# A hybrid attention and expert block on one core: low parts of the output weights on VectorE alone, first linear-attention states and read-out inside the attention loop

## The chip, the cores and the metric

The kernel runs on one core of a Trainium2 chip. The metric is the device time in microseconds of one execution. PE is TensorE, ACT is ScalarE, DVE is VectorE, POOL is GpSimd and SP is SyncE, whose queue issues most of the loads.

## What is computed

One layer of a residual block over 1024 tokens of width 1024, all in 32-bit floats:

```python
u = rms_norm(h, g1);  proj = u @ w_in          # split into sq sk sv | gq gk gv gr glr
sb = stick_breaking_attention(norm(sq), norm(sk), sv)     # 8 heads x 64, causal, blocks of 128 queries
sb = rms_norm(sb, sb_out_norm_g)
# gated linear attention, 4 heads, key 64, value 128, chunks of 64 tokens:
S = exp(total) * S + k_dec.T @ v ;  o = q @ S              # S is carried from chunk to chunk
go = rms_norm(o, gla_out_norm_g) * silu(gr)
h = h + concat(sb, go) @ w_out
h = h + hierarchical_moe(rms_norm(h, g2))                  # 32 experts, two for each token
```

## The kernel before, in words

Each engine has a program of its own, written in order by hand; only semaphores tie them together. A large product is made from high and low parts, so that one product is three matmuls: for each weight W, `W_h = round(W)` is made by ScalarE and `W_l = W - W_h` by VectorE or GpSimd.

**Stages.** (1) Norm and transposes of x, then the projection in 40 units. (2) The attention loop: 48 steps (`steps_z`, NZ = 48), n = 0 to 47. Query tile i has 4 pairs of heads, and one (i < 4) or two steps a pair; tile 7 has steps 40 to 47, each 512 keys wide. Software pipelining runs the engines some steps apart: in iteration n TensorE does `scores(n)`, `turn_a(n-2)` and `values(n-3)`; ScalarE two sigmoids of step n and the copy of the probabilities of step n-2; VectorE two scans and one product of step n. In the gaps `fill` makes the query and gate columns (12 units, the last one in iteration 39). (3) The output projection, 8 tiles of 128 tokens: each with 8 steps k of 6 matmuls (`three` for two halves). Between the steps stand small works: the state of the linear attention (`keys_values(t, c)` on TensorE, `next_state(n)` on VectorE, n = 2t + c), its read-out (`read_state`), the transposes of its output (`turn_gla`) and of the attention output (`turn_sb`), and of the tile before `turn_h`, `route` and `rank_tile`. (4) The experts, 32 or more blocks: six pieces of 1 MiB of weights each, split into high and low parts by ScalarE (`high`, line 1419) and VectorE (`low_piece`, line 1527), then 96 matmuls.

**Output weights.** SyncE loads w_out in four parts into raw slots 1, 2, 3 and again 1 (`load_wo`, line 421), once the fill is done. ScalarE makes wo_h in iterations 41, 42, 43 and 45 (`WO_SPLIT`). GpSimd makes wo_l of parts 0 and 1 (line 582: multiply two rows by a gain; line 584: one subtraction of 128 x 2048), VectorE that of parts 2 and 3 (`wo_low`, line 1611: two fused instructions of 128 x 1024).

**End of the loop.** Bank 6 collects the attention output of every tile; `values` of a new tile waits until ScalarE's `evict_o` has emptied it. After the loop TensorE runs: keys_values(0, 0), keys_values(0, 1), both read_state(0, c), turn_sb(0), keys_values(1, 0), turn_gla(0), keys_values(1, 1), and then the projection of tile 0. VectorE answers with next_state(0), next_state(1), go_mean(0), and so on. GpSimd waits for the last scores, clears the three states, then loads gv_in 0 and 1 and gate_in and scales all eight rows of the attention output (`norm_sb`, line 602).

**Weight pieces.** There are six raw slots and two extra, and six split slots. SyncE issues pieces 0 to 5 behind the stores of tiles 0 to 5 (waits `v_ready`), then waits for all scatters of rows by expert (`own_scattered`, line 469), then issues piece 6 and so on, each when the piece that held its slot has been split (`ew_l_ready`). Pieces 12 and 13 lie where the rows of the last tiles lay. After tile 7 the engines build block 0 from rows in memory and rows still at hand (`first_rows`, `add_rows`) and run gate_up(0).

**In tile 7 of the projection** (w = 7 on VectorE and ScalarE) stand the routing of tile 6 (`take_logits`, `choose`, `rank_tile(6)` behind k = 6, `place_tile(6)`). ScalarE makes the high parts of pieces 0 and 1 after it, VectorE the low part of piece 0 between place_tile(6) and `add_h(7)` (line 1698).

## Time and profile before

| | |
|---|---|
| three runs, median (lowest to highest) | 1273.97 us (1273.42 to 1276.81) |
| the profiled execution | 1275.61 us |
| its span, first to last instruction | 1273.8 us |
| mean granted TensorE clock | 0.971 of full |
| busy: PE, DVE, ACT, POOL | 1192.8, 871.7, 734.2, 297.8 us |
| chain that ended last: PE, DMA, DVE, ACT, issue | 68%, 17%, 6%, 5%, 3% |

The rows below come from that one execution. A timeline line gives start and duration in microseconds, engine, line of the kernel, operation, out<-in, shapes and count; what stands in brackets is the idle time of the engine before it and what ended that. A granted clock of 1.00 is 2.4 GHz, 0.50 is 1.2 GHz. Where two instructions of an engine overlap in a group, the group's time is the stretch they cover.

### The profile page before, as it was taken

To read this page: it belongs to the slowest core of one execution; us is meant where nothing else is said; L and a number is where in the kernel's file an instruction comes from. 1 tells how busy PE (TensorE), PEld (TensorE's weight loads), DVE (VectorE), ACT (ScalarE), POOL (GpSimd) and SP (SyncE) were. 2 spreads that over 40 slices of the span, in tenths; PEclk is the share of its full clock that TensorE was granted. 3 is DMA by queue.
4 is the path that set the end of the run, shared out by engine and by line. 5 is a ranking of instruction groups with operands and counts; after the bars stand their busy time and mean duration, and the time that the engine had idled before them with its cause. 6 is when DMAs were issued, how large, how long until landed. Compare 5 with 4: busy or idle time off the path is not lost.

```text
span 1273.8 us, 17673 instructions
## 1 busy us (share of the span) xinstructions
PE 1192.8 (94%) x6172; PEld 976.1 (77%) x6172; DVE 871.7 (68%) x987; ACT 734.2 (58%) x894; POOL 297.8 (23%) x256
## 2 busy tenths in 40 slices
PE   4999999999999968999978999999999999999993
PEld 3897777877767746777866888888788888888883
DVE  5721212267556696577668999888888888888880
ACT  4532222266455583223245887887778777878870
POOL 3400000010000074033232333334344222232210
PEclk9999999999999987999988999999999999999997
DMA  7145432020000122356639999999999999999961
GB/s 255 43 162 219 151 139 108 1 67 17 18 12 23 57 93 88 111 209 231 254 135 385 371 378 383 377 372 372 368 374 378 370 379 374 372 379 390 379 241 15
DMA packets 67828, 288.12 MB, mean 226 GB/s; under 512 B 13008, under 2 KB 20193, under 8 KB 43202
## 3 DMA queue, kind: packets, MB, share of 16 engines
q1 hardware_dynamic: 51538, 238.30, 49.1%
q0 software_dynamic: 10864, 30.29, 8.6%
q10 hardware_dynamic: 5376, 18.88, 3.8%
q8 instruction: 30, 0.49, 0.2%
q14 instruction: 20, 0.16, 0.0%
HBM read 242.79 MB, written 48.25 MB: 228 GB/s over the span
## 4 chain that ended last, share of the span: by engine, by line
PE 68%; DMA 17%; DVE 6%; ACT 5%; issue 3%; SPq 0%; ACTq 0%; POOL 0%; POOLq 0%; DVEq 0%
PE banks L746 17%; DMA raw<-in_expert_w_up 16%; PE banks L747 16%; PE banks L748 16%; PE banks L886 4%; DVE ew_l L1527 3%; PE banks L853 3%; ACT ew_h L1419 2%; PE banks L870 2%; PE banks L974 1%; DVE tails L1630 1%; PE banks L1066 1%; PE banks L919 1%; PE banks L933 1%; DMA x_in<-in_x 1%
## 5 line engine op out<-in xcount | busy, mean ns | idle before, releaser
L1527 DVE TENSOR_TENSOR ew_l<-raw,ew_h 128x2048 fp32r<-128x2048 f32 x192 | 437.9, 2290 | 64.1 <-ACT ew_h L1419 62.9
L1419 ACT ACTIVATE ew_h<-raw 128x2048 fp32r<-128x2048 f32 x192 | 368.1, 1919 | 122.2 <-DMA raw<-in_expert_w_up 50.5
L746 PE MATMUL banks<-ew_h,xb_h 128*128 128x512 f32 x512 | 204.2, 399 | 12.2 <-issue 6.8
L748 PE MATMUL banks<-ew_h,xb_l 128*128 128x512 f32 x512 | 201.1, 393 | 0.0
L747 PE MATMUL banks<-ew_l,xb_h 128*128 128x512 f32 x512 | 201.0, 393 | 0.0
L1630 DVE TENSOR_TENSOR_SCAN tails<-tails 128x512 f32<-128x512 f32 (+3 forms) x96 | 103.2, 1117 | 63.8 <-ACT tails L1314 63.7
L746 PE MATMUL banks<-win_h,u_h 128*128 128x512 f32 (+1 forms) x320 | 123.7, 387 | 0.1
L746 PEld LDWEIGHTS banks<-ew_h,xb_h 128*128 128x128 f32 x512 | 97.3, 190 | 34.2 <-issue 14.5
L747 PE MATMUL banks<-win_l,u_h 128*128 128x512 f32 (+1 forms) x320 | 120.4, 376 | 0.0
L748 PE MATMUL banks<-win_h,u_l 128*128 128x512 f32 (+1 forms) x320 | 119.9, 375 | 0.0
L748 PEld LDWEIGHTS banks<-ew_h,xb_l 128*128 128x128 f32 x512 | 97.1, 190 | 20.9
L747 PEld LDWEIGHTS banks<-ew_l,xb_h 128*128 128x128 f32 x512 | 97.1, 190 | 19.3
L746 PE MATMUL banks<-ew_h,a_h 128*128 128x512 f32 x256 | 103.1, 403 | 2.2 <-DVE a_l L1527 2.2
L747 PE MATMUL banks<-ew_l,a_h 128*128 128x512 f32 x256 | 100.6, 393 | 0.0
L748 PE MATMUL banks<-ew_h,a_l 128*128 128x512 f32 x256 | 100.6, 393 | 0.0
L695 POOL DMA_INDIRECT out_dram<-y_row,scatter_row x32 | 46.6, 1457 | 175.6 <-issue 175.6
L574 POOL TENSOR_TENSOR z_l<-z_raw,z_h 128x1024 fp32r<-128x1024 f32 x6 | 14.6, 2440 | 306.1 <-ACT z_h L1250 306.1
L1314 ACT ACTIVATE tails<-banks 128x1024 f32<-128x1024 f32 (+3 forms) x48 | 39.3, 818 | 74.7 <-PE banks L857 59.4
L685 POOL DMA_INDIRECT xb<-rows_dram,gather_idx x30 | 65.7, 2189 | 52.3 <-issue 50.4
L886 PEld LDWEIGHTS banks<-v_s,prob 128*128 128x128 f32 x576 | 73.5, 199 | 5.1 <-issue 2.2
L886 PE MATMUL banks<-v_s,prob 128*128 128x64 f32 x576 | 72.2, 277 | 2.0 <-ACT o_sb L1302 2.0
L746 PEld LDWEIGHTS banks<-win_h,u_h 128*128 128x128 f32 x320 | 61.3, 192 | 12.8 <-issue 2.9
(242 smaller groups left out, 2023.7 us busy)
## 6 DMA issues: line engine op xcount, KB each, us to landing
raw<-in_expert_w_gate SPq DMA_DIRECT2D x64, 1024.0 KB, 12.0
raw<-in_expert_w_up SPq DMA_DIRECT2D x64, 1024.0 KB, 8.4
raw<-in_expert_w_down SPq DMA_DIRECT2D x64, 1024.0 KB, 12.7
rows_dram<-zero_rows ACTq DMA_DIRECT2D x8, 2048.0 KB, 7.6
win_raw<-in_w_in SPq DMA_DIRECT2D x16, 512.0 KB, 5.3
x_in<-in_x SPq DMA_DIRECT2D x8, 512.0 KB, 9.9
raw<-in_w_out SPq DMA_DIRECT2D x4, 1024.0 KB, 5.9
h_row<-in_x SPq DMA_DIRECT2D x8, 512.0 KB, 6.3
```

The lines of the kernel that those rows point to most:

```text
L685: pool.indirect_dma_start(out=xb[0:n, :], out_offset=None, in_=rows_dram, in_offset=bass.IndirectOffsetOnAxis(ap=gather_idx[0:n, :], axis= ...
L695: pool.indirect_dma_start(out=out_rows, out_offset=bass.IndirectOffsetOnAxis(ap=scatter_row[0:n, 0:1], axis=0), in_=y_row[0:n, :], in_offs ...
L746: mm(ps, lh, rh, start=start, stop=False)
L747: mm(ps, lh, rl, start=False, stop=False)
L748: return mm(ps, ll, rh, start=False, stop=stop)
L853: last = mm(z[h], q_t[row, u["i"], u["pair"], :], k_t[row, u["pair"], u["lo"]:u["lo"] + u["w"]], start=True, stop=True)
L870: last = nc.tensor.transpose(bank[4 + h][:, P * j:P * j + P], beta[n % 3][:, h, P * j:P * j + P], ident[:, :])
L886: last = mm(bank[6][:, SB_DIM * hd:SB_DIM * (hd + 1)], prob[n % 2][:, h, P * j:P * j + P], v_s[:, u["lo"] // P + j, SB_DIM * hd:SB_DIM * ( ...
L1314: A(tails[u["row"] % 2][:, :, u["col"]:u["col"] + u["w"]], z, ACT.Sigmoid, scale=-1.0).then_inc(c_done, 1)
L1419: A(ew_h[slot % SPLIT][:, :], raw[raw_slot][:, :], ACT.Copy).then_inc(ew_h_ready, 1)
L1527: return V.tensor_tensor(dst, src, high.bitcast(fp32), SUB)
L1630: last = V.tensor_tensor_scan(out=part, data0=part, data1=part, initial=1.0 if u["top"] else row[:, h, c1:c1 + 1], op0=MUL, op1=ALU.min)
```

## The change

1. **wo_l on VectorE alone.** The GpSimd loop is gone; VectorE makes all four parts. The parts are in raw slots 1, 2, 1, 2; ScalarE and VectorE split them in iterations 41, 42, 44 and 45. SyncE loads two parts at once and the others when VectorE is done with the slot. Raw slot 3's memory is thus free and takes the three states and gv_in 0.
2. **Linear attention in the loop.** keys_values(0, 0) goes behind iteration 44 of TensorE, keys_values(0, 1) behind 45 (it waits for next_state(0)), both read_state(0, c) behind 47. next_state(0) and next_state(1) stand at the ends of iterations 45 and 46 on VectorE. These use bank 6; the attention output of the last tile is collected in bank 7. ScalarE does go_square(0) and go_rstd(0) in iterations 48 and 49 and evict_o(7) after sb_high(0).
3. **Start of the projection.** Before tile 0 stand only turn_sb(0), turn_gla(0) and keys_values(1, 0); keys_values(1, 1) goes behind k = 1, read_states(1) behind k = 2, keys_values(2, 0) behind k = 3.
4. **GpSimd** clears the states and loads gv_in 0 when the fill is done; norm_sb(t + 1) is done in turn t of its loop, after load_gate(t), instead of all at once.
5. **First pieces.** The high and the low part of piece 0 are made in turn w = 7, the low part ahead of take_logits(6). SyncE's wait for the scatters moves from before piece 6 to before piece 12; piece 5 waits for the last read-out (g_o), as its slot holds the states.

```diff
-        WO_SPLIT = {FILL_LAST + d: n for n, d in enumerate((2, 3, 4, 6))}
+        WO_SPLIT = {FILL_LAST + d: n for n, d in enumerate((2, 3, 5, 6))}
+        WO_SLOT = (1, 2, 1, 2)
...
@@ SyncE
-            for n in range(3):
+            for n in range(2):
                 load_wo(n)
             store_gate(2 * GLA_HEADS - 1)
-            sp_e.wait_ge(wo_l_ready, 1)
-            load_wo(3)
+            for n in range(2, 4):
+                sp_e.wait_ge(wo_l_ready, n - 1)
+                load_wo(n)
...
+                if t == 5:
+                    sp_e.wait_ge(g_o, 2 * TILES)
                 if t < 6:
                     load_piece(raw_slot(t), gate_up(t // 4, t % 4))
...
-            for k in range(2):
-                sp_e.wait_ge(own_scattered[k], 32 * TILES // 2)
             for j in range(2, 6):
                 sp_e.wait_ge(ew_l_ready, j - 1)
...
                 if m == 12:
                     sp_e.wait_ge(x_turned, 1)
                     for k in range(2):
+                        sp_e.wait_ge(own_scattered[k], 32 * TILES // 2)
                         sp_e.wait_ge(v_stored[k], 16 * TILES // 2)
@@ GpSimd
-            for n in range(2):
-                pool.wait_ge(wo_h_ready, n + 1)
...
-                nc.gpsimd.tensor_tensor(wo_l[:, 2 * n:2 * n + 2, :], src[:, :, :], wo_h[:, 2 * n:2 * n + 2, :].bitcast(fp32),
-                                        SUB).then_inc(wo_l_ready, 1)
...
-            pool.wait_ge(qk_done, NZ)
-            for i in range(3):
+            pool.wait_ge(fill_done, FILL_UNITS)
+            nc.gpsimd.memset(state[2][:, :, :], 0.0)
+            for i in range(2):
                 last = nc.gpsimd.memset(state[i][:, :, :], 0.0)
             last.then_inc(prepared, 1)
             for i in range(2):
                 pool.wait_ge(gv_stored[i], 16 * TILES // 2)
+            load_gv(0)
+            pool.wait_ge(qk_done, NZ)
+            load_gv(1)
             pool.wait_ge(gate_stored, 16 * 2 * GLA_HEADS)
-            load_gv(0)
-            load_gv(1)
             load_gate(0)
-            for t in range(TILES):
-                norm_sb(t)
+            norm_sb(0)
+            norm_sb(1)
...
                 load_gate(t)
+                if t + 1 < TILES:
+                    norm_sb(t + 1)
@@ TensorE
+            GLA_EARLY = {NZ - 4: lambda: keys_values(0, 0), NZ - 3: lambda: keys_values(0, 1), NZ - 1: lambda: read_states(0)}
...
                 if n >= 3:
                     values(n - 3)
+                if n in GLA_EARLY:
+                    GLA_EARLY[n]()
...
-            keys_values(0, 0)
-            keys_values(0, 1)
-            for c in range(2):
-                read_state(0, c)
             turn_sb(0)
+            turn_gla(0)
             keys_values(1, 0)
-            turn_gla(0)
-            keys_values(1, 1)
...
+                    if t == 0 and k == 1:
+                        keys_values(1, 1)
+                    if k == (0 if t else 2) and t + 1 < TILES:
+                        read_states(t + 1)
...
-                    if k == 2 and t + 2 < TILES:
+                    if k == (2 if t else 3) and t + 2 < TILES:
                         keys_values(t + 2, 0)
@@ ScalarE
+                    go_square(0)
+                if n == NZ + 1:
+                    go_rstd(0)
...
-            go_square(0)
-            go_rstd(0)
             sb_high(0)
+            evict_o(TILES - 1, NZ - 1)
+            go_high(0)
...
+                if w == TILES - 1:
+                    act.wait_ge(g_mixed, TILES)
+                    high(0, 0, raw_slot(0), raw_count(0), guard=False)
@@ VectorE
-                if WO_SPLIT.get(n, 0) >= 2:
+                if n in WO_SPLIT:
                     wo_low(WO_SPLIT[n])
+                if NZ - 3 <= n < NZ - 1:
+                    next_state(n - (NZ - 3))
...
                 if r >= 0:
                     norm_h(r)
+                if w == TILES - 1:
+                    low_piece(0, 0, raw_slot(0))
+                if r >= 0:
                     take_logits(r)
...
             place_tile(TILES - 2)
-            low_piece(0, 0, raw_slot(0))
             add_h(TILES - 1)
```

## Rows read from the trace of the kernel before

**Rows 1.** Timeline, VectorE in the last attention steps: start us, us, what.
```profile
450.57 1.23 DVE L1635 TENSOR_TENSOR beta<-beta,tails 128x1024 f32<-128x1024 f32 x1
...
456.89 0.67 DVE L1623 TENSOR_REDUCE o_ms<-o_sq 128x8 f32<-128x512 f32 x1
...
458.19 7.12 DVE L1630 TENSOR_TENSOR_SCAN tails<-tails 128x512 f32<-128x512 f32 x2 [0.63 <-ACT tails L1314]
...
469.74 6.64 DVE L1630 TENSOR_TENSOR_SCAN tails<-tails 128x512 f32<-128x512 f32 x2
...
481.19 2.47 DVE L1611 SCALAR_TENSOR_TENSOR wo_l<-raw,mix_gain,wo_h 128x1024 fp32r<-128x1024 f32 x2
...
487.09 2.45 DVE L1630 TENSOR_TENSOR_SCAN tails<-tails 128x512 f32<-128x512 f32 x2
...
489.58 1.23 DVE L1635 TENSOR_TENSOR beta<-beta,tails 128x1024 f32<-128x1024 f32 x1
...
496.11 1.43 DVE L1659 SCALAR_TENSOR_TENSOR state<-state,gstat,banks 64x128 f32<-64x128 f32 x4 [5.30 <-PE banks L919]
```

**Rows 2.** The same timeline, GpSimd.
```profile
457.70 4.53 POOL L584 TENSOR_TENSOR wo_l<-raw,wo_h 128x2048 fp32r<-128x2048 f32 x1
...
492.24 7.03 POOL L602 TENSOR_TENSOR o_sb<-o_sb,o_rs 128x512 f32<-128x512 f32 x7 [3.85 <-ACT o_rs L1338]
```

**Rows 3.** The same timeline, TensorE and one ScalarE eviction.
```profile
477.70 1.97 PE L870 MATMUL banks<-ident,beta 128*128 128x128 f32 x8 [6.97 <-DVE beta L1635]
...
482.90 2.08 PE L853 MATMUL banks<-k_t,q_t 64*128 64x512 f32 x4
...
485.03 1.03 ACT L1314 ACTIVATE tails<-banks 128x1024 f32<-128x1024 f32 x1 [4.30 <-PE banks L853]
...
486.39 1.90 PE L886 MATMUL banks<-v_s,prob 128*128 128x64 f32 x16
...
495.40 0.65 PE L919 MATMUL banks<-gv_in,k_dec 64*64 64x128 f32 x8
...
507.35 0.79 PE L746 MATMUL banks<-wo_h,mix_h 128*128 128x512 f32 x1
```

**Rows 4.** Busy time and granted clock: us, PE, PEld, DVE, ACT, POOL, PEclk, DMA share, GB/s.
```profile
477.00:486.00 9.00, 8.30 (x33) 6.68 (x34) 8.93 (x9) 2.00 (x3) 0.95 (x3) 0.50 0.00 0
```

**Rows 5.** Timeline, a read-out inside tile 0 of the output projection.
```profile
510.12 1.09 PE L933 MATMUL banks<-state,gq_t 128*64 128x256 f32 x8
```

**Rows 6.** Timeline of the last tiles before the experts, 628 to 668 us.
```profile
635.65 0.22 DVE L1715 SCALAR_TENSOR_TENSOR grp_logits<-banks,stat,router_bias 128x4 f32<-128x4 f32 x1 [2.49 <-PE banks L974]
...
641.68 2.33 DVE L1527 TENSOR_TENSOR ew_l<-raw,ew_h 128x2048 fp32r<-128x2048 f32 x1
...
643.93 1.27 DVE L1698 TENSOR_TENSOR h_row<-h_row,banks 128x512 f32<-128x512 f32 x2
```

**Rows 7.** Waits of the DMA queue of SyncE, 640 to 720 us: total, times, longest.
```profile
SPq L469 <- DMA rows_dram<-v_row,dest: 19.4, 1, 19.4
```

**Rows 8.** Stretches of 4 us: length, granted clock, DMA share, GB/s.
```profile
658.00:662.00 4.00, 1.00 0.00 0
...
670.00:674.00 4.00, 0.95 0.94 359
```

**Rows 9.** Raw weight loads issued from 462 to 463 us: issue to landing.
```profile
DMA to landing us min/median/max: 4.7/4.7/4.7
```

**Rows 10.** Raw weight loads issued from 712 to 718 us: issue to landing.
```profile
DMA to landing us min/median/max: 7.3/7.3/7.3
```

**Rows 11.** Raw weight loads issued from 856 to 874 us: issue to landing.
```profile
DMA to landing us min/median/max: 12.4/12.9/13.4
```

**Rows 12.** The chain that ended last, whole span: start us, us, what.
```profile
699.42 0.88 PE banks L1066 x8
...
823.69 0.88 PE banks L1066 x8
...
1133.89 0.88 PE banks L1066 x8
```

More of the change, by code:

```diff
@@ L1607, in wo_low @@
                 dve.wait_ge(wo_h_ready, n + 1)
-                src = raw[(1, 2, 3, 1)[n]][:, :].rearrange("p (k n) -> p k n", n=D)
+                src = raw[WO_SLOT[n]][:, :].rearrange("p (k n) -> p k n", n=D)
                 for kk in range(2):
@@ L1612, in wo_low, with next_state @@
                                                   in1=wo_h[:, k, :].bitcast(fp32), op0=MUL, op1=SUB)
-                last.then_inc(wo_l2_ready, 1)
+                last.then_inc(wo_l_ready, 1)
+            def next_state(n):
+                t, c = divmod(n, 2)
+                kv_bank = bank[7 if t else 6]
+                dve.wait_ge(g_kv, n + 1)
+                if n == 0:
+                    dve.wait_ge(prepared, STATES)
+                else:
+                    dve.wait_ge(g_state, n)
+                if n >= 3:
+                    dve.wait_ge(g_o, n - 2)
+                for p in range(2):
+                    for h in range(2):
+                        r, col = slice(64 * h, 64 * h + 64), slice(GLA_V * h, GLA_V * (h + 1))
+                        last = V.scalar_tensor_tensor(out=state[n % 3][r, p, col], in0=state[(n - 1) % 3][r, p, col],
+                                                      scalar=gstat[r, t, 2 * p + c:2 * p + c + 1],
+                                                      in1=kv_bank[r, GLA_V * p:GLA_V * (p + 1)], op0=MUL, op1=ADD)
+                last.then_inc(g_state, 1)
             dve.wait_ge(unit_done, UNITS)
@@ L1771, in place_tile, with low_piece @@
                 dve.wait_ge(dest_ready, 2 * (t + 1))
-            next_state(0)
-            next_state(1)
+            def low_piece(count, slot, raw_slot):
+                dve.wait_ge(ew_h_ready, count + 1)
+                low(ew_l[slot % SPLIT][:, :], raw[raw_slot][:, :], ew_h[slot % SPLIT][:, :]).then_inc(ew_l_ready, 1)
             go_mean(0)
+            go_norm(0)
+            sb_low(0)
+            go_gate(0)
+            go_low(0)
+            next_state(2)
             dve.wait_ge(o_squared, TILES)
             V.reduce_sum(o_ms[:, TILES - 1, :], heads(o_sq[:, :]), axis=AX.X).then_inc(o_mean, 1)
-            go_norm(0)
-            sb_low(0)
-            next_state(2)
-            go_gate(0)
-            go_low(0)
             next_state(3)
```

155 lines of the change are left out of this document (65 added, 90 removed).

## The prediction, made before the changed kernel was run

> **What bounds the kernel now.** I read the chain that ended last first, because it says which wait counts in which stage, then the timeline around the places that the diff touches, then the waits and landings of the loads. Three stages have three limits. In the last attention steps the chain runs over VectorE: a step costs it two scans and a product, 3.72 us from 487.09 to 490.81, yet two pairs of scans took 7.12 and 6.64 us where a free pair takes 2.45 [rows 1]. Each lies on a 4.5 us GpSimd subtraction for wo_l (one of two in [rows 2]). TensorE stands idle behind that for 6.97 us and then runs at half clock (0.50 from 477 to 486 us [rows 3, 4]). From the last values matmul, 495.4, to the first output-projection matmul, 507.35, is 11.9 us of short dependent work for one tile [rows 3]. The projection itself is bound by TensorE. The experts are bound by TensorE at first, 17.75 us a block from 699.42 to 823.69 (7 blocks), then by the weight loads, 18.25 us a block from 823.69 to 1133.89 (17 blocks), with the load as the link before the split [rows 12]. Ahead of the experts the DMA engines stand still (0.00 at 658 us [rows 8]) while SyncE waits 19.4 us for row scatters before it issues piece 6 [rows 7].
>
> **The change part by part.** All sums are against the profiled execution: span 1273.8, 1275.61 in all, which is 1.6 above the median 1273.97 of the three runs. I take the difference off the median.
>
> *VectorE in the loop.* I start at 451.80, the end of the product of step 41 [rows 1]. To the product of step 47, at 490.81, it took 39.0 us: six steps at 3.72 (22.3), two wo_low at 2.47 (4.9), one head sum 0.67, and 11.1 of hindrance, of which the two long scan pairs are 4.7 + 4.2. Without GpSimd's part the hindrance goes. The work becomes six steps 22.3, four wo_low 9.9, head sum 0.7, two state updates at 1.43 [rows 1] 2.9: 35.8 us. The raw reloads for wo_low 2 and 3 are hidden: they are issued at 454.3 and 460.5, land 4.7 later [rows 9] and are wanted by VectorE at 468.6 and 474.8; if they came 5 us late they would cost what remains, nothing.
>
> *The new wait.* After step 45 TensorE waits for next_state(0), which VectorE reaches only after scan, product and wo_low(3) of that step. Queued behind the wait is scores(46), and for that wait ScalarE's eviction and VectorE's scan of step 46. The ledger puts next_state(0) at 477.3 to 478.7. TensorE's last work before is values(42), ended about 467.5, so it idles 11 us, and I take the half clock that followed the 6.97 us idle. Then keys_values(0,1) 1.0 (a row of 0.65 at full clock [rows 3], 1.0 at half), scores 2.08 and its mask 0.3, eviction 1.03 [rows 3]: VectorE starts step 46 at 483.2, 4.5 us of bubble. Step 46 and next_state(1) end at 488.3. scores(47) waits on TensorE for turn_a(44) 1.97 and values(43), 3.3 at half clock (1.90 at full [rows 3]), so it starts at 487.4 and its eviction ends at 489.5: bubble 1.2. The product of step 47 ends at 493.2, 2.4 later than before, although 11.1 us of hindrance are gone. No row shows which clock TensorE has after 11 us idle: at full clock both bubbles shrink to 3.0 in all and the loop ends some 4 us earlier than put here, at half clock to its end it is rival 3; I go by the nearest row, 6.97 us idle and then half clock to about 486.
>
> *End of the loop.* Before, from scores(47) at 482.90 to 495.4 TensorE worked without a gap for 12.5 us, 1.6 of it excess of the half clock. Now 487.4 + 10.9 + 1.1 for read_states(0) (1.09 [rows 5]) = 499.4. ScalarE puts go_square(0) before the last copy of probabilities, 0.6, mostly under values(46). The loop ends 4.0 later.
>
> *Hand-over to the projection.* Gone from it are both keys_values of tile 0, both state updates, the read-out, square, mean and scale. Left, by the rows that exist: turn_sb(0) 0.5 to 0.6 (four transposes; eight took 1.97 at half clock), its copy 0.6 and evict_o(7) 1.1 (one and two evictions of 512 columns; 1024 took 1.03), keys_values(1,0) 0.65 [rows 3], and 0.15 of hand-overs: 3.1 us, so the first projection matmul comes at 502.5 instead of 507.35: **4.9 us**. GpSimd's three memsets, moved to the end of the fill, stand in free time. load_gv(0) is issued 40 us earlier; load_gate(0) and norm_sb(0) stand behind load_gv(1) as before. norm_sb(0) is ready at 497, turn_sb(0) wants it at 499.4.
>
> *Tile 0 of the projection.* keys_values(1,1) (0.65) moves in, read_states(1) goes behind k=2. The state of chunk 3 is ready when it is read, the one of chunk 4 about 0.3 late. Against that stands less half clock: the first six matmuls took to 510.12, 2.8 us, and cost 1.4 at full clock [rows 3, 5]. From +0.9 to -0.9; I take 0.
>
> *Tile 7.* high(0) and low(0) of the first expert go before take_logits(6), which started at 635.65; low takes 2.33 and ends at about 637.1, so the logits come 1.4 late, and rank_tile(6) holds TensorE's last six matmuls by 1.3. But add_h(7), which waited for that low piece from 641.68 to 643.93 [rows 6], starts at about 642.8: **1.1 us** won, between -1.3 and 2.3. SyncE's wait for g_o = 16 at t = 5 costs nothing: the last read-out lies in tile 6 before norm_h(5).
>
> *Piece loads.* SyncE no longer waits for the scatters. Pieces 6 and 7 go out at about 648 and 650 instead of 668.7, piece 8 at 664, piece 9 at 669 (its split has not moved). Three pieces of 1.05 MB at the 359 GB/s of 670 to 674 us [rows 8] are 8.8 us of DMA time taken out of the queue. That is not the gain: the ring of raw buffers allows no more issues ahead, and by 712 us a load lands 7.3 us after issue [rows 10] where one into idle engines took 4.7 [rows 9]. Only 2.6 us of backlog are there to remove; after that the engines go idle. Later the landing grows to 12.9 [rows 11] and the blocks stretch; 17 blocks lost 17 x (18.25 - 17.75) = 8.4 us [rows 12], and a backlog 2.6 smaller puts the onset off by as much. I take **2.4**, between 0 and 8.4.
>
> Sum: 4.9 + 0 + 1.1 + 2.4 = 8.4 us, 1273.97 - 8.4 = **1265.6**.
>
> **A rule on ports.** The long scans waited until GpSimd's subtraction had ended, and a GpSimd multiplication beside them did far less. The Trainium skill, "SBUF — State Buffer", section "Who interferes with whom", says why: a VectorE instruction with two SBUF inputs and a GpSimd one that reads SBUF exclude each other for a whole instruction. By that rule, the trace agrees on the scans. It also speaks against this change, which moves six norm_sb into the projection: rival 4.
>
> **The rivals.**
> 1. *The head start of the loads is lost* (0.20): transfers drain to the same backlog by the point where blocks stretch. For it: the DMA share is already 0.94 at 670 us [rows 8], so the megabytes behind meet a queue all the same. 1273.97 - 6.0 = 1268.0.
> 2. *The head start counts in full* (0.10), since bound by loads is bound by their first byte. Against it: the 7.3 us landing. 1273.97 - 6.0 - 8.4 = 1259.6.
> 3. *Slower: the half clock stays* (0.07). TensorE idles 11 us instead of 7 in the loop. If it does not return by 487, each microsecond at the lower level costs about half of one; the gain is gone when it lasts some 17 us longer, and lasting 27 longer, to tile 0, costs 13.5: 1279.1. Against it: after 6.97 us idle the half clock was over by 486.39, where 16 values matmuls took 1.90 again [rows 3].
> 4. *GpSimd blocks VectorE in the projection* (0.10). Before, all but the last norm_sb ran in one stretch at 492.24, 7.03 us for seven [rows 2]; now norm_sb 2 to 7 stand one to a tile, 1.0 each: up to 6 us, 1271.6, no measurable change. Against it: the state updates at 496.11 ran at full speed beside them [rows 1], and TensorE, not VectorE, is full in this stage. The skill's page named above would make it so for go_low and norm_h, which have two SBUF inputs.
> 5. *The loop does not give what it promises* (0.08): the wait for next_state(0) costs twice the 5.7 of bubble that I put, as the pipeline of three engines must fill again. 1265.6 + 5.7 = 1271.3.
>
> **How the numbers follow.** Forecast 0.45, with 1263 to 1268 as its own range (tile 0 by 0.9 either way, tile 7 by 1). About 0.3%, 3.8 us, is what a measurement can tell from no change: 1270.2 and 1277.8 are the marks. Faster: forecast, rivals 1 and 2, and 0.02 of 4 and 5, 0.77. Same: the rest of 4 and 5, 0.16. Slower: rival 3, 0.07. The range 1258.5 to 1271.5 takes in rivals 1, 2 and 5 and the full-clock case (some 1261.6), and leaves out rival 3, the upper end of 4, and what I have not seen, 0.2 in all.
>
> **What would show it.** Scan pairs in steps 42 to 47 all near 2.45 and no subtraction on GpSimd; TensorE idle about 11 us before keys_values(0,1); the first projection matmul near 502.5; add_h(7) without a low piece before it; DMA engines busy from 648 to 656 us; landings near 5 us at block 2, with blocks stretching some five later than now. The prediction is wrong if the loop ends after 503, if loads land in 7 us again at block 2, or if the tiles of the projection grow longer than before.

## The result, and the profile after

The changed kernel takes 1265.62 us, the median of 5 runs (1261.56 to 1266.81), against 1273.97 for the kernel before beside it, also 5 runs (1272.15 to 1276.81): a ratio of 0.993, 95% interval 0.9909 to 0.9951. The forecast was 1265.6. Its sum agrees with the result, but most of its terms do not. Two large ones were wrong in opposite directions, and a microsecond and a half came from a stage that nobody changed. One execution of experiment e9 below took 1974.52 us at a granted clock of 0.557 and is left out of its median and ratio.

The profiled execution took 1266.81 us, with a span of 1265.1 and a mean granted clock of 0.976 (before: 1275.61, 1273.8, 0.971). The rest of this document compares stages by the starts of the same instructions in both traces: first scores matmul of step 40, first matmul of the output projection, its last matmul of wo_h with mix_h (two more follow it, up to 0.9 us later, and then add_h of tile 7 can start), first matmul of `first_rows`, `turn_rows` of block 2, last matmul. What the stages sum to in the profiled execution, and what the prediction had for each:

| stage | before | after | difference | forecast |
|---|---|---|---|---|
| start to step 40 | 442.12 | 440.50 | -1.6 | 0 |
| step 40 to the first projection matmul | 65.23 | 56.78 | -8.45 | -4.9 |
| projection, tile 0 | 16.01 | 15.61 | -0.4 | 0 |
| projection, tiles 1 to 6 | 103.10 | 107.29 | +4.2 | 0 (rival 4: up to +6) |
| tile 7, and to `first_rows` | 25.04 | 23.42 | -1.6 | -1.1 |
| `first_rows` to block 2 | 47.76 | 48.73 | +1.0 | 0 |
| block 2 to the last matmul | 556.84 | 555.00 | -1.8 | -2.4 |

**The start.** The difference arises ahead of step 0 of the loop, where nothing is changed, and most of it in one place: TensorE ran at half clock from 209.6 to 213.0 us in the kernel before, and at full clock at the same work in the changed one. Windows as in [rows 4], kernel before, then changed:

```profile
209.00:213.00 4.00, 4.00 (x12) 3.11 (x11) 0.42 (x1) 0.31 (x2) 0.00 (x0) 0.57 0.38 127
```

```profile
208.00:212.00 4.00, 3.95 (x19) 3.38 (x20) 0.43 (x1) 0.47 (x3) 0.00 (x0) 1.00 0.69 196
```

**The end of the loop.** VectorE of the changed kernel, timeline (start, duration, what), to be read against [rows 1]:

```profile
458.98 2.45 DVE L1653 TENSOR_TENSOR_SCAN tails<-tails 128x512 f32<-128x512 f32 x2
...
474.53 1.42 DVE L1633 SCALAR_TENSOR_TENSOR state<-state,gstat,banks 64x128 f32<-64x128 f32 x4
480.56 2.34 DVE L1653 TENSOR_TENSOR_SCAN tails<-tails 128x512 f32<-128x512 f32 x2 [4.60 <-ACT tails L1329]
...
485.65 2.46 DVE L1653 TENSOR_TENSOR_SCAN tails<-tails 128x512 f32<-128x512 f32 x2
```

All pairs of scans take 2.33 to 2.46 us where two had taken 7.12 and 6.64, and GpSimd does no arithmetic until 491 us. The state update ends at 475.95, and the idle 4.60 ahead of the scans of step 46 is the bubble (forecast 4.5). The scans of step 47 follow on the second update without a hole; the forecast had 1.2 there. TensorE, against [rows 3]:

```profile
476.01 1.12 PE L904 MATMUL banks<-gv_in,k_dec 64*64 64x128 f32 x8 [10.30 <-DVE state L1633]
...
479.25 1.25 PE L865 MATMUL banks<-ident,beta 128*128 128x128 f32 x8
480.34 1.90 PE L884 MATMUL banks<-v_s,prob 128*128 128x64 f32 x16
...
494.38 0.61 PE L960 MATMUL banks<-ident,o_sb 128*128 128x128 f32 x4
...
497.28 0.50 PE L741 MATMUL banks<-wo_h,mix_h 128*128 128x512 f32 x1
```

TensorE idles 10.30 us for the state update (forecast 11), and keys_values(0, 1) behind it takes 1.12 instead of 0.65. From 479.25 on the groups are short again: 1.25 for a turn that takes 1.97 at half clock, then 1.90 for a `values` of 16. The granted clock by windows, in the columns of [rows 4]:

```profile
470.00:474.00 4.00, 0.00 (x0) 0.00 (x0) 3.97 (x4) 0.00 (x0) 0.00 (x0) 0.50 0.00 0
474.00:478.00 4.00, 1.99 (x10) 1.22 (x12) 1.91 (x5) 0.00 (x0) 0.00 (x0) 0.50 0.00 0
478.00:482.00 4.00, 4.00 (x30) 2.94 (x26) 1.44 (x2) 2.50 (x3) 0.00 (x0) 0.79 0.00 0
```

The clock is down for about 10 us, but TensorE works at it only from 476.0 to some 479.5. In the kernel before it worked 8.3 us at that level, 477.7 to 486, behind a hole of 6.97 us [rows 3, 4].

**The projection.** Waits of TensorE for other engines from tile 1 to the end of tile 6 (total, times, longest):

```profile
PE banks L989 <- DVE chosen_any L1749: 3.6, 4, 0.9
```

In the kernel before nothing was waited for in these tiles. L989 is `rank_tile`, which wants `chosen_any` (line 1749), the last result of `choose`. One such place on the timeline, VectorE:

```profile
547.48 1.56 DVE L1734 TENSOR_SCALAR r_small<-iota,r_small 128x4 f32<-128x4 f32 x1
...
550.91 0.18 DVE L1749 TENSOR_TENSOR chosen_any<-chosen 128x32 bf16<-128x32 bf16 x1
```

and GpSimd:

```profile
547.95 1.06 POOL L593 TENSOR_TENSOR o_sb<-o_sb,o_rs 128x512 f32<-128x512 f32 x1
```

A VectorE comparison of 4 elements a partition takes 1.56 us: it ends with the `norm_sb` of GpSimd (549.01) that started after it. It does so four times, 1.2 us ahead of the first matmul of tiles 2 to 5 (548.71 for this one), and each of these tiles takes 18.43 to 18.51 us instead of 17.41 to 17.49.

**Tile 7.** VectorE in the last tiles, against [rows 6]:

```profile
628.39 2.29 DVE L1532 TENSOR_TENSOR ew_l<-raw,ew_h 128x2048 fp32r<-128x2048 f32 x1 [1.49 <-ACT ew_h L1363]
...
636.01 1.29 DVE L1706 TENSOR_TENSOR h_row<-h_row,banks 128x512 f32<-128x512 f32 x2
```

The low piece now stands ahead of the logits, and add_h(7) starts 0.97 us after the projection's last matmul of wo_h with mix_h (635.04) instead of 3.31.

**The loads.** Waits of SyncE's queue (total, times, longest), against [rows 7]:

```profile
SPq L449 <- DVE ew_l L1532: 54.7, 13, 12.3
SPq L460 <- DVE v_row L1717: 12.7, 1, 12.7
```

The issues on the timeline:

```profile
641.36 2.40 SPq L449 DMA_DIRECT2D raw<-in_expert_w_up  x2
656.10 5.33 SPq L449 DMA_DIRECT2D raw<-in_expert_w_down  x2
```

The 19.4 us for the scatters are gone; pieces 6 and 7 go out from 641.36 instead of 668.69 (the forecast had 648). Stretches against [rows 8]: length, busy times, clock, DMA share, GB/s.

```profile
642.00:646.00 4.00, 4.00 (x19) 4.00 (x19) 2.55 (x14) 2.11 (x3) 1.52 (x1) 0.50 0.99 338
650.00:654.00 4.00, 3.43 (x22) 3.31 (x22) 2.02 (x13) 0.18 (x1) 0.14 (x1) 0.97 0.04 16
694.00:698.00 4.00, 4.00 (x19) 3.30 (x18) 4.00 (x5) 3.25 (x4) 1.78 (x2) 1.00 0.44 184
```

The DMA engines are busy at 642 us, idle at 650 (0.04), and at 694 to 698 again idle more than half of the time, where the kernel before shows 1.01. So they do catch up, as forecast. The chain that ended last, against [rows 12]:

```profile
692.50 0.88 PE banks L1068 x8
...
816.77 0.88 PE banks L1068 x8
...
1124.88 0.88 PE banks L1068 x8
```

The first seven blocks take 17.75 us each, the seventeen that follow 18.12 (before 18.25). The first block that stretches is number 14, where it was 12; the forecast had the onset some five blocks later.

### The profile page after: what moved, and what is told of

Same layout as the page of the kernel before. It is cut to its first block, busy times and chain, and to the rows that moved or that the text cites. A ratio compares the mean times of both kernels' runs of the same rounds, so it can differ in the third digit from the quotient of the medians.

```text
span 1265.1 us, 17671 instructions
## 1 busy us (share of the span) xinstructions
PE 1183.9 (94%) x6172; PEld 970.1 (77%) x6172; DVE 871.3 (69%) x991; ACT 735.4 (58%) x894; POOL 283.5 (22%) x250
## 4 chain that ended last, share of the span: by engine, by line
PE 72%; DMA 10%; DVE 8%; ACT 4%; issue 4%; POOL 1%; SPq 0%; POOLq 0%; ACTq 0%; DVEq 0%
PE banks L741 19%; PE banks L743 18%; PE banks L742 18%; DMA raw<-in_expert_w_up 8%; PE banks L884 4%; PE banks L848 3%; DVE ew_l L1532 2%; PE banks L865 2%; ACT ew_h L1363 2%; DVE tails L1653 1%; PE banks L1068 1%; PE banks L980 1%; DMA raw<-in_expert_w_down 1%; PE banks L904 1%; DMA x_in<-in_x 1%
## 5 line engine op out<-in xcount | busy, mean ns | idle before, releaser
L1653 DVE TENSOR_TENSOR_SCAN tails<-tails 128x512 f32<-128x512 f32 (+3 forms) x96 | 94.0, 1021 | 67.0 <-ACT tails L1329 66.7
L742 PEld LDWEIGHTS banks<-ew_l,xb_h 128*128 128x128 f32 x512 | 97.5, 190 | 19.4
L680 POOL DMA_INDIRECT xb<-rows_dram,gather_idx x30 | 62.7, 2090 | 54.1 <-issue 54.1
L884 PEld LDWEIGHTS banks<-v_s,prob 128*128 128x128 f32 x576 | 70.5, 191 | 3.0 <-ACT prob L1340 0.2
L884 PE MATMUL banks<-v_s,prob 128*128 128x64 f32 x576 | 69.6, 270 | 0.1
## 6 DMA issues: line engine op xcount, KB each, us to landing
x_in<-in_x SPq DMA_DIRECT2D x8, 512.0 KB, 10.2
```

The source lines that it names most:

```text
L680: pool.indirect_dma_start(out=xb[0:n, :], out_offset=None, in_=rows_dram, in_offset=bass.IndirectOffsetOnAxis(ap=gather_idx[0:n, :], axis= ...
L742: mm(ps, lh, rl, start=False, stop=False)
L884: last = mm(o_bank[:, SB_DIM * hd:SB_DIM * (hd + 1)], prob[n % 2][:, h, P * j:P * j + P], v_s[:, u["lo"] // P + j, SB_DIM * hd:SB_DIM * (h ...
L1653: last = V.tensor_tensor_scan(out=part, data0=part, data1=part, initial=1.0 if u["top"] else row[:, h, c1:c1 + 1], op0=MUL, op1=ALU.min)
```

## The experiments

Each kernel below was traced once and timed in several rounds beside the kernel before. Single executions of one kernel differ by 4 to 6 us either way, so an edit worth 2 us is read in the stages of the traces. a0 to e7 ran on one chip, e8 and e9 on a second, f1 to f3 on a third, each beside the kernel before, so kernels of different groups are compared by their ratios. The projection column ends at that last matmul of wo_h with mix_h. One table for all (us; the ratio is to the kernel before, with its interval):

| kernel | median, ratio | 40 to proj. | projection | to `first_rows` | to block 2 | to the end |
|---|---|---|---|---|---|---|
| before | 1272.6 to 1274.7 | 65.23 | 133.27 | 10.88 | 47.76 | 556.84 |
| changed | 1265.62, 0.9930 | 56.78 | 137.76 | 8.56 | 48.73 | 555.00 |
| a0 the changed kernel again | 1266.17, 0.9936 (0.9913 to 0.9959) | 56.87 | 137.71 | 8.56 | 48.81 | 559.01 |
| e1 norm_sb first | 1259.03, 0.9891 (0.9874 to 0.9908) | 57.23 | 134.06 | 7.97 | 47.23 | 550.89 |
| e2 wait for scatters | 1265.91, 0.9946 (0.9926 to 0.9965) | 57.17 | 137.78 | 8.32 | 47.54 | 557.23 |
| e3 piece 0 back | 1263.99, 0.9931 (0.9912 to 0.9949) | 57.41 | 137.08 | 11.30 | 47.61 | 555.04 |
| e4 part 1 alone | 1267.05, 0.9949 (0.9924 to 0.9974) | 57.90 | 133.22 | 10.84 | 47.50 | 554.57 |
| e6 wait a step later | 1259.23, 0.9884 (0.9855 to 0.9912) | 52.69 | 137.76 | 7.41 | 47.97 | 554.28 |
| e7 three edits | 1259.39, 0.9880 (0.9848 to 0.9912) | 52.70 | 133.56 | 7.15 | 46.54 | 553.53 |
| e8 norm_sb before gate | 1256.90, 0.9856 (0.9820 to 0.9893) | 57.04 | 133.54 | 7.64 | 47.60 | 555.02 |
| e9 e7 with the wait | 1256.98, 0.9863 (0.9822 to 0.9905) | 52.69 | 133.54 | 7.30 | 48.00 | 555.14 |
| f1 e7 again | 1258.99, 0.9863 (0.9829 to 0.9896) | 58.53 | 136.05 | 7.93 | 47.32 | 554.49 |
| f2 e9 again | 1259.22, 0.9881 (0.9845 to 0.9917) | 56.33 | 133.58 | 7.24 | 48.05 | 554.97 |
| f3 e6 and e8 | 1255.00, 0.9836 (0.9805 to 0.9866) | 52.70 | 133.60 | 8.57 | 47.76 | 558.19 |

**a0: the changed kernel again,** no edit.

> The changed kernel as it is, once more, as the yardstick of this group of runs. All theories: within 2 us of 1265.6. The first trace shows 1.4 to 1.6 us less than the kernel before already at steps 0 to 40 of the attention loop, where nothing is changed. If that is chance, this run's offset at step 40 differs from it; if it belongs to the change, it comes back at 1.6.

Up to block 2 the stages repeat within 0.1 us. Behind it the trace is 4.0 longer: block 11 alone took 3.9 longer than the others, once. Start to step 40 differs in every trace, by 0.9 to 4.2 us less than in the traced kernel before, and it is there already at the scores of step 0, where nothing was changed; in the trace of the changed kernel it is 1.6. It goes by how long TensorE's clock was at half in this stage: 6.8 us in the eight traces that reach step 40 at 438.0 to 438.7, 10.2 in the four at 440.0 to 440.9 (changed and a0 among them), 13.7 in the two at 441.2 and 442.1 (e3 and before). That part of the 8.7 us is chance.

**e1: norm_sb first.** All but the last `norm_sb` in one stretch ahead of tile 0, as before.

```diff
             norm_sb(0)
             norm_sb(1)
+            load_gv(2)
+            for t in range(2, TILES - 1):
+                norm_sb(t)
...
-                if t + 1 < TILES:
+                if 3 <= t + 1 < TILES:
                     load_gv(t + 1)
                 load_gate(t)
-                if t + 1 < TILES:
-                    norm_sb(t + 1)
+                if t == 1:
+                    norm_sb(TILES - 1)
```

> GpSimd scales rows 2 to 6 of the attention output before the projection again, and row 7 in its first turn. Theory (rival 4 of the prediction was real): tiles 2 to 5 of the projection took 18.5 us instead of 17.4 because norm_sb held up a small VectorE instruction in the routing of the tile before, which TensorE waits for. Then these tiles take 17.4 again, TensorE's 3.6 us of waits for chosen_any vanish, and the time falls by 4.2 us to about 1261.4. Rival: the tiles are longer for another reason (the earlier start brings them against the row transfers): tiles stay at 18.5 and the time within 1 us of the changed kernel.

The projection is back to 134.06, and the comparison takes 0.41. TensorE waits for no other engine in tiles 1 to 6. The comparison:

```profile
545.02 0.41 DVE L1737 TENSOR_SCALAR r_small<-iota,r_small 128x4 f32<-128x4 f32 x1
```

The median falls by 7 us, of which this stage is 3.7. The last stage, 4.1 shorter in this trace, is not explained by the edit: 2.5 of it is less stretching of the blocks, and 1.6 lies in the last block, 31.4 us instead of 33.0, without the stretch of half clock that the changed kernel has there (1240.8 to 1244.3).

**e8: norm_sb one place earlier in the tile.** e1 takes all but one of GpSimd's `norm_sb` out of the projection. Here they stay in the tiles, but ahead of load_gate(t), so that they do not wait for g_mixed and do not fall into `choose`.

```diff
                     load_gv(t + 1)
-                load_gate(t)
                 if t + 1 < TILES:
                     norm_sb(t + 1)
+                load_gate(t)
```

> The changed kernel with one line moved: in GpSimd's turn of tile t, norm_sb(t + 1) stands ahead of load_gate(t) instead of behind it. It then no longer waits for g_mixed of tile t, and so no longer falls in the middle of choose, but follows load_gv(t + 1). From the changed kernel: the projection from its first matmul to its last took 137.8 us, four of its tiles 18.4 to 18.5 instead of 17.4; r_small (L1734) took 1.56 us beside a norm_sb of 1.06 and 0.23 where it stood alone. Theory A (what costs is that norm_sb meets one short VectorE instruction inside choose, on which rank_tile waits behind the first matmuls of a tile): the tiles are back at 17.4 to 17.6, the projection at 133.5 to 134.5, r_small at 0.23 in all tiles, median 4 lower than the changed kernel, 1261 to 1263. Theory B (a norm_sb anywhere in a projection tile costs about its own length, whatever it meets): the tiles stay at 18.2 to 18.5, the projection at 137 to 138, median 1265 to 1267. In between, 135 to 136: it meets another instruction of VectorE on which a matmul waits.

Theory A holds: 133.54, the comparison 0.43, and no wait in tiles 1 to 6. The median, 1256.90, lies below the 1261 to 1263 that was expected; what makes up the rest is not known. The `norm_sb` of a tile now meets v_row, with two SBUF inputs. VectorE's takes 1.87 instead of 1.28, GpSimd's 1.88 instead of 1.06, and nobody waits for either. VectorE, then GpSimd, on the timeline:

```profile
538.51 1.87 DVE L1717 SCALAR_TENSOR_TENSOR v_row<-h_row,stat,gain 128x1024 f32<-128x1024 f32 x1
```

```profile
539.39 1.88 POOL L593 TENSOR_TENSOR o_sb<-o_sb,o_rs 128x512 f32<-128x512 f32 x1
```

So it is not the amount of GpSimd's work that cost 4.2 us but the one instruction that it met, because TensorE stood behind it. In all five traces of kernels with the changed kernel's order of GpSimd (changed, a0, e2, e3, e6) the comparison takes 1.55 or 1.56 us four times and tiles 2 to 5 take 18.4 to 18.5; in the nine others it never takes over 0.43, and these tiles take 17.4 to 17.5.

**e2: the wait for the scatters back,** ahead of piece 6 on SyncE.

```diff
+            for k in range(2):
+                sp_e.wait_ge(own_scattered[k], 32 * TILES // 2)
             for j in range(2, 6):
                 sp_e.wait_ge(ew_l_ready, j - 1)
```

> Only the wait for the row scatters before piece 6 is put back. Theory of the prediction: the head start of three pieces is worth only the backlog that it removes, 2.4 us (the two first traces show 1.8 between block 2 and the end), so the time rises by 1.8 to 2.4 us. Rival 1: nothing, the same time within 1 us. Rival 2: the whole head start counts, 8 us more.

SyncE waits 19.2 us again:

```profile
SPq L472 <- DMA rows_dram<-v_row,dest: 19.2, 1, 19.2
```

The last stage is 2.2 longer than in the changed kernel's first trace and 1.8 shorter than in its second. Medians are equal (1265.91, 1266.17). One trace could not decide it, so the pair was made again on a better kernel: e9, f1, f2 below.

**e3: low and high of piece 0 back behind place_tile(6).**

```diff
-                if w == TILES - 1:
-                    low_piece(0, 0, raw_slot(0))
...
             place_tile(TILES - 2)
+            low_piece(0, 0, raw_slot(0))
             add_h(TILES - 1)
```

> Only piece 0 goes back: its high part after tile 7's turn, its low part between place_tile(6) and add_h(7). Theory: add_h(7) waits for the low piece again, +2.3 us there, and tile 7 is 0.7 shorter, so first_rows starts 1.6 us later and the time rises by 1 to 1.6 us. The head start of piece 6 hangs on piece 0 too, but SyncE is held by the stores of tile 7 until later, so nothing more. Rival: the order does not matter, as piece 1 and piece 2 have to be split anyway: same time within 0.5 us.

VectorE, the low piece and add_h(7) behind it, as in [rows 6]:

```profile
636.86 2.33 DVE L1531 TENSOR_TENSOR ew_l<-raw,ew_h 128x2048 fp32r<-128x2048 f32 x1
639.11 1.27 DVE L1705 TENSOR_TENSOR h_row<-h_row,banks 128x512 f32<-128x512 f32 x2
```

From the end mark of the projection to `first_rows` 11.30 against 8.56, +2.7; the projection 0.7 shorter, as rank_tile(6) no longer comes late. The move is worth 2.1 us in this pair of traces; between before and changed it was 2.3 - 0.7 = 1.6. The medians do not show it: e3's 1263.99 is lower than a0's 1266.17, within the spread of either.

**e4: part 1 alone.** The kernel before, with the low parts of w_out on VectorE, two slots and the new order of loads; nothing else.

```diff
-        WO_SPLIT = {FILL_LAST + d: n for n, d in enumerate((2, 3, 4, 6))}
+        WO_SPLIT = {FILL_LAST + d: n for n, d in enumerate((2, 3, 5, 6))}
+        WO_SLOT = (1, 2, 1, 2)
...
-            for n in range(2):
-                pool.wait_ge(wo_h_ready, n + 1)
...
-                if WO_SPLIT.get(n, 0) >= 2:
+                if n in WO_SPLIT:
                     wo_low(WO_SPLIT[n])
```

> The kernel before with one part of the change alone: all four parts of wo_l on VectorE, in slots 1, 2, 1, 2, split in iterations 41, 42, 44 and 45; nothing else moved. Theory: the two scan pairs fall from 7.1 and 6.6 to 2.45 us, the loop's VectorE work from the product of step 41 to that of step 47 falls from 39.0 to about 33, TensorE no longer idles 7 us, and the loop ends about 6 us earlier; the 11.9 us up to the projection stay. Time 1273.97 - 6 = about 1268. Rival: the scans were long for another reason than the subtraction on GpSimd (their own inputs, the transfers of w_out): then they stay long, the two more wo_low add 5 us, and the time rises to about 1278.

The stage takes 57.90: 7.3 of the 8.45 us are there without moving a single step of the linear attention. The scans are free: of the two pairs that had been long, steps 43 and 44, the first takes 2.45 (at 456.68) and the second 2.33. TensorE no longer stands for 7 us at one of them; the second pair, and TensorE's two largest waits from step 41 to tile 0:

```profile
460.30 2.33 DVE L1620 TENSOR_TENSOR_SCAN tails<-tails 128x512 f32<-128x512 f32 x2
```

```profile
PE banks L909 <- DVE state L1649: 2.8, 2, 1.5
PE banks L860 <- DVE beta L1625: 2.4, 2, 1.6
```

What was moved into the loop brings 1.1 us in the changed kernel: it takes dependent steps out of the hand-over (11.9 us from the last `values` to the projection before [rows 3], 2.9 now) and pays nearly all of it back in the loop, with the hole of 10.30. The 7.3 and 1.1 come from one trace of each kernel, and that of e4 is the fastest of its 12 executions (1261.63, up to 1273.98). By the medians e4 alone is 6.0 us faster than the kernel before, with an interval that overlaps the changed kernel's: how the gain divides is known to about a microsecond or two.

**e6: the wait one step later.** keys_values(0, 1) behind iteration 46, next_state(1) in 47, the read-out behind 48.

```diff
-            GLA_EARLY = {NZ - 4: lambda: keys_values(0, 0), NZ - 3: lambda: keys_values(0, 1), NZ - 1: lambda: read_states(0)}
+            GLA_EARLY = {NZ - 4: lambda: keys_values(0, 0), NZ - 2: lambda: keys_values(0, 1), NZ: lambda: read_states(0)}
...
-                if NZ - 3 <= n < NZ - 1:
-                    next_state(n - (NZ - 3))
+                if n in (NZ - 3, NZ - 1):
+                    next_state((n - (NZ - 3)) // 2)
```

> The changed kernel, but TensorE meets its wait for next_state(0) one step later: keys_values(0,1) behind iteration 46, next_state(1) at the end of 47 and the read-out behind 48. Theory: the 10.3 us idle of TensorE and the 4.6 us that VectorE waits for step 46 come from the place of this wait, ahead of scores(46). With scores(46) ahead of it VectorE runs on into step 46, and the loop ends about 3 us earlier: about 1262.6. Rival: the loop is bound by TensorE's backlog after the idle time all the same, and the read-out stands later, so that go_square, go_norm and turn_gla(0) come later: same time within 1 us.

```profile
473.99 0.65 PE L904 MATMUL banks<-gv_in,k_dec 64*64 64x128 f32 x8 [3.24 <-DVE state L1633]
```

```profile
472.52 1.42 DVE L1633 SCALAR_TENSOR_TENSOR state<-state,gstat,banks 64x128 f32<-64x128 f32 x4
473.97 2.34 DVE L1653 TENSOR_TENSOR_SCAN tails<-tails 128x512 f32<-128x512 f32 x2
```

The scores of step 46 are on their way before the wait, so VectorE goes from the state update straight into the scans of 46, and 47 follows. TensorE idles 3.24 us instead of 10.30. The stage takes 52.69, 4.1 less than in the changed kernel: the price of the wait's place, of which the bubble of 4.60 is the visible part. In two later traces, f1 and f2, the half clock takes this gain back.

**e7: three edits.** e6 and e1 together, and next_state(0) ahead of wo_low(3) in VectorE's iteration 45.

> The changed kernel with rows 2 to 7 scaled early (as in e1), the wait one step later (as in e6), and next_state(0) ahead of wo_low(3) in step 45, so that TensorE is released 2.5 us earlier. If the three add up: 4.2 + 3 + about 1.5 below the changed kernel, 1257. If the places overlap (rival): no better than the better of e1 and e6, about 1261.

The gains of e6 and e1 add up stage by stage, 52.70 and 133.56; the third edit, put at 1.5 us, brings nothing (52.69 without it). The span is 1249.2, 16 less than the changed kernel's. The median, 1259.39, is no lower than that of either edit alone. The runs behind it show why.

**e9: e7 with the wait for the scatters,** the edit of e2 on it. **f1, f2: e7 and e9 once more,** side by side.

> The version with all three edits (the norm_sb first, the wait for the first state one step later, the state update ahead of wo_low), with SyncE's wait for the scatters put back ahead of piece 6. Measured on the stretch of the expert blocks 2 to 31 beyond 17.755 us each, summed: 8.3 to 9.3 us in the three kernels with the wait that were traced, 6.4 to 7.2 in four of five without it. Theory (the head start removes only the backlog in front of the blocks): the sum is 8.5 to 9.3 here, 1.5 to 2.5 above the version without the wait, the blocks start to stretch at number 11 or 12, and the median is 1260 to 1263 against 1259.4. Rival (the difference seen so far is chance, or came from something other than this wait): the sum is 6 to 7.5 and the onset at 13 or later. A difference of 2 us does not show in one pair of medians; the trace decides.

> The version with all three edits once more, beside the next kernel, in one comparison. Without SyncE's wait the blocks 2 to 31 stretched by 7.2 us in its first trace, and by 7.2 with the wait, so the head start of the loads is in doubt. Theory (it is worth the backlog, about 2 us): the sum is 6.4 to 7.5 here again, and the median lies 1 to 3 us below that of the next kernel. Rival (it is worth nothing): both sums lie anywhere between 6.5 and 9 with no order, and the medians are within 1 us or the other way round.

> The same with SyncE's wait for the scatters ahead of piece 6. Theory: stretch of blocks 2 to 31 of 8.3 to 9.3, median 1 to 3 us above the kernel before this one. Rival: 6.5 to 9, median within 1 us of it or lower.

*The head start.* What the blocks 2 to 31 take beyond 17.755 us each, summed: with the wait 8.9 (before), 9.3 (e2), 8.3 (e4), 7.2 (e9), 7.1 (f2), mean 8.2; without it 7.1 (changed), 11.2 (a0, with its one block of 3.9), 4.6 (e1), 7.1 (e3), 6.4 (e6), 7.2 (e7), 7.1 (e8), 6.6 (f1), 10.3 (f3), mean 7.5. The theory wanted 8.3 or more from e9 and f2; they gave 7.2 and 7.1. The medians have no order either: e9 is below e7, f2 above f1, each by less than their spread. What remains is a difference of 0.7, less than two traces of one kernel differ by. Yet the engines do run empty without the wait, and do not with it. Stretches of f1 and f2, as above:

```profile
690.00:700.00 10.00, 10.00 (x47) 8.34 (x46) 9.11 (x7) 8.45 (x9) 2.04 (x2) 1.00 0.65 231
...
710.00:720.00 10.00, 10.00 (x47) 8.37 (x46) 8.96 (x7) 8.55 (x7) 3.98 (x4) 1.00 1.01 369
```

```profile
690.00:700.00 10.00, 10.00 (x47) 8.34 (x46) 8.73 (x7) 8.60 (x8) 2.16 (x2) 1.00 0.99 354
...
710.00:720.00 10.00, 10.00 (x45) 8.26 (x44) 8.51 (x5) 9.10 (x8) 3.56 (x2) 1.00 1.00 348
```

The pause in f1 is over by 710 us. The blocks begin to stretch at number 11 or 12 in all five traces with the wait, and at 13 to 15 in six of the nine without (a0's one long block 11 left out), at 10 to 12 in three: a shift of some blocks, often, but hardly a difference in the sum. Of the forecast's 2.4 us some 0.7 is borne out, and none of it is shown; it stays open between 0 and 2.

The landings show what becomes of the head start. Raw weight loads of f1, issued from 695 to 700 us and from 701 to 706, then those of f2, issued from 692 to 698, issue to landing:

```profile
DMA to landing us min/median/max: 4.9/5.0/5.2
...
DMA to landing us min/median/max: 7.0/7.3/7.6
```

```profile
DMA to landing us min/median/max: 6.9/7.4/7.8
```

Without the wait two loads meet idle engines and land in 5 us, as forecast, and the next already take as long as with it. The same two short landings, 4.9 to 5.3 us, stand in a0, e1 and e3.

*The clock.* e7 and f1 are one program. Their stage from step 40 to the projection took 52.70 and 58.53 us, their projection 133.56 and 136.05: 8.3 us apart. Granted clock behind the hole in e7, then in f1 (third number from the end):

```profile
470.00:476.00 6.00, 4.91 (x21) 3.08 (x22) 5.90 (x8) 1.74 (x2) 1.33 (x2) 0.54 0.03 7
476.00:482.00 6.00, 5.10 (x41) 4.96 (x40) 5.89 (x8) 3.74 (x5) 0.00 (x0) 0.89 0.34 90
```

```profile
478.00:490.00 12.00, 11.28 (x56) 10.05 (x54) 5.76 (x9) 4.91 (x8) 7.57 (x8) 0.52 0.32 112
490.00:501.00 11.00, 10.14 (x42) 8.57 (x42) 3.96 (x8) 2.71 (x6) 1.63 (x2) 0.50 0.11 35
```

The work, e7 first:

```profile
484.24 3.68 PE L887 MATMUL banks<-v_s,prob 128*128 128x64 f32 x32
...
490.67 0.50 PE L744 MATMUL banks<-wo_h,mix_h 128*128 128x512 f32 x1
```

```profile
486.31 6.93 PE L887 MATMUL banks<-v_s,prob 128*128 128x64 f32 x32
...
496.85 0.79 PE L744 MATMUL banks<-wo_h,mix_h 128*128 128x512 f32 x1
```

In e7 the clock was down from 470 to 477 us, behind a hole of 4.03, with some 6 us of work in it. In f1 it fell only at 478, after holes of 0.84 and 1.55 us, and stayed at 0.50 for 23 us in which TensorE was busy for 21.4; the same `values` of 32 took 6.93 us instead of 3.68. In f2 it was down from 472.7 to 489.7 with 16.6 us of work in it, in e9, its twin, for 6 us of work, both behind a hole of 4.0. In f2:

```profile
472.00:488.00 16.00, 14.89 (x68) 12.11 (x68) 11.96 (x15) 5.81 (x7) 3.10 (x4) 0.52 0.29 100
488.00:500.00 12.00, 10.73 (x79) 9.07 (x77) 5.34 (x10) 4.72 (x10) 6.59 (x8) 0.93 0.14 44
```

This is rival 3 of the prediction, in 2 of 13 traces with the change or part of it, and it fits that the median does not follow the trace of e7: the two fastest executions of e7 had a mean granted clock of 0.983 and 0.978, the two slowest 0.972 and 0.970. The order of the changed kernel gave 56.78 to 57.41 in all its six traces (changed, a0, e1, e2, e3, e8); the later wait gave 52.69 or 52.70 four times and 56.33 and 58.53. What makes the clock return sooner or later was not found. Two things stand beside it in the traces. Both long stretches are in kernels with the third edit of e7, which also gave 52.70 twice; e6 and f3, without it, gave 52.69 and 52.70. And seven traces (e1, e2, e4, e6, e8, f1, f3) have an earlier stretch of half clock, some 6.8 us from 454 or 458 on with TensorE busy throughout, behind a hole of 1.7 to 2.0 us; the kernel before has one of 3.4 us there, the other six none. It makes TensorE later, so the next hole is shorter: 7.13 instead of 10.30 in e1, e2 and e8, 0.84 instead of 4.03 in f1. Neither is shown to be the cause.

**f3: e6 and e8,** the later wait and norm_sb ahead of load_gate, nothing more.

> The changed kernel with the wait for the first state one step later and norm_sb ahead of load_gate in GpSimd's turn; neither of the other two edits. If the two add up, the stretch from step 40 to the first projection matmul is 52.7 us as with the first alone, the projection 133.5 to 134 as with the second alone, the execution 8 us shorter than the changed kernel's in the stages up to the experts, and the median 1256 to 1259. If they disturb each other (norm_sb moved onto the reordered hand-over), the projection is at 135 to 138.

52.70 and 133.60: they add up. 1255.00, ratio 0.9836, is the lowest median of all, with its interval (0.9805 to 0.9866) clear of the changed kernel's (0.9909 to 0.9951). It is below the 1256 to 1259 that was expected. Against e6, e7, e8, e9, f1 and f2 the intervals overlap, and no order among these is claimed.

## Why the prediction was right in its sum

**VectorE in the loop: right.** No long scan is left, and the ledger held: next_state(0) ends at 475.95, with the 1.6 us of the earlier start 477.6, where 477.3 to 478.7 stood. e4 shows the step by itself, 7.3 us in its trace and 6.0 by the medians, and that it carries most of the gain. The prediction did not price it by itself, and so did not see that the rest of the move was worth little.

**The new wait: mechanism right, the clock mis-sized.** Hole 10.30 (11 forecast), bubble 4.60 (4.5). The wrong term is the one that rested on a single row, how long the half clock lasts: put at "to about 486" after [rows 3, 4], it went on for 3.5 us of work, to some 479.5. The scores of step 47 began at 482.16, or 483.8 with the start's 1.6 added, where 487.4 stood. Of these 3.6 us, 2.4 are turn_a(44) and values(43) at full clock, 2.9 us instead of 5.3, and 1.1 lie ahead of them, as the sum had gone by the late end of its own 477.3 to 478.7. With that the bubble before step 47 (1.2) is gone too. From there on the loop ran as forecast (12.2 us, 12.0 put): it was done at 494.4, or 496.0, where 499.4 stood. These 3.4 us and 0.2 of the hand-over are the 3.55 by which the stage beat 4.9. The prediction's other bound, full clock, "some 4 us earlier", was nearly the truth. e6 shows that the wait itself, priced here and accepted, was avoidable: 4.1 us, in the traces where the clock returned soon.

**Hand-over: right.** From the last `values` to the projection 2.9 us, forecast 3.1.

**Tile 0: right,** -0.4 in a range of 0.9 either way. **Tile 7: right in both of its parts,** +0.7 (forecast 1.3) and -2.3 (forecast 2.3 to 2.4); e3 undoes both.

**The projection: the step that failed.** GpSimd's `norm_sb` in the tiles was costed at nothing, since state updates ran at full speed beside it [rows 1] and TensorE was full. Rival 4, at 0.10, is what happened, 4.2 us, and with it one of the three signs by which the prediction said that it would be wrong: longer tiles. Its reason was only half right. It looked for long VectorE instructions with two SBUF inputs, go_low and norm_h; what was held was one of 0.2 to 0.4 us, because it began just ahead of GpSimd's and on the chain to `rank_tile`. The evidence against it came from another instruction: the state updates, whose second tensor comes from a PSUM bank. The Trainium skill, "SBUF — State Buffer", section "Who interferes with whom", lists copies, casts and `tensor_scalar` as able, when their operands allow it, to enter a mode that takes the port shared with GpSimd, beside the instructions with two SBUF inputs. By that wider rule the comparison, a `tensor_scalar` with one SBUF input, is held too; the trace agrees (1.56 us). The prediction had used the narrower half of the rule.

**The loads: not shown.** 2.4 us forecast; the profiled execution gives 1.8 here, but the pairs e2, e9 and f2 do not hold that up. That the wait ends, that the engines run empty and that loads then land in 5 us was right. The step that failed is that the cleared backlog stays cleared: two loads land in 5 us, the third takes 7 or more again (f1, e1), and what is left in the sum of the blocks is 0.7 us, smaller than chance. Rival 1 (1268.0), a backlog that builds up again, was nearer in this term. `first_rows` to block 2, +1.0, was not in the sum; the granted clock was 0.79 from 655 to 693 us, against 0.87 in the same stretch before (662 to 700), and the stage varies from 46.5 to 48.8 over all traces.

Put together: 3.55 better up to the projection, 4.2 worse in it, 1.6 of luck at the start, 1.0 lost ahead of block 2, and 0.3 better in the rest. The forecast time was right because these cancel: that is luck. The terms are those of one trace of each kernel, 8.7 us apart; the medians are 8.35 apart.

## What to carry to other kernels

Before work is moved onto an engine that shares a port, look not for the longest instruction that it may meet but for the ones that another engine's first matmul waits for: 1 us of GpSimd at the wrong place cost 1 us a tile, and 0.0 one place earlier in the same turn. When dependent steps are moved into a loop, put the wait behind the issue of the step that keeps the bound engine fed: one iteration later was worth 4.1 us in four traces of six. And where one edit of a change can stand alone, price it alone: here it carried 7.3 of 8.45 us in its trace, 6.0 of 8.35 by the medians.

## What the runs showed of the hardware

- A VectorE TENSOR_SCALAR of 128 x 4, 0.23 to 0.43 us by itself, took 1.55 to 1.56 in four tiles, to the end of a GpSimd multiplication of 1.06 that started 0.47 after it by the profile.
- TensorE's half clock behind a hole is not a fixed price. It went on for 3.5 us of work behind 10.3 us idle (changed) and for 8.3 behind 6.97 (before); one program showed 6 us of it and over 21 (e7, f1), another 6 and 16.6 (e9, f2), and in f1 it began with no hole over 1.55 us in the 6 us ahead of it. Over the stages concerned one program came out 8.3 us apart.
- In the stage ahead of step 40, which no edit changes up to its last microseconds, the half clock made up 6.8, 10.2 or 13.7 us, and the stage took 438.0 to 442.1 us in that order.
- DMA engines that had run empty for some microseconds at 690 us were full again at 720: two loads landed in 4.9 and 5.2 us, the next two in 7.0 and 7.6 (f1), and the blocks behind stretched as much as without the pause, to within 1 us.
